# The first weight sums of the twice split feed-forward stages: from GpSimd arithmetic to accumulating DMAs, with the second sums on VectorE

## The chip, the cores and the metric

The kernel runs on one core of one Trainium2 chip. The core has TensorE (matrix products), VectorE (elementwise, the profile's DVE), ScalarE (ACT), GpSimd (POOL) and SyncE (SP, which here issues DMAs). The metric is the device time of one execution in microseconds (us).

## The reference

The program is a transformer of two kinds of block on 512 tokens of width 1024, all in float32. Its first block has two layers, and each layer ends in a gated feed-forward network:

```python
D_FF = 2816
f = rmsnorm(h, ln_ffn_pre[layer])
f = (jax.nn.silu(f @ w_ffn_gate[layer]) * (f @ w_ffn_up[layer])) @ w_ffn_down[layer]
h = h + rmsnorm(f, ln_ffn_post[layer])
```

The change concerns the two products `f @ w_ffn_gate` and `f @ w_ffn_up`, in both layers: two stages of the program. A third feed-forward network, in the second block, is computed by other code and isn't touched.

## The kernel before, in words

The function `ffn_up_quarters` makes one stage. The 2816 columns of each of the two weights are taken 256 at a time, in 11 units (`UNITS`), numbered 0 to 10. A unit has two tiles, each of 1024 rows by 256 columns: one from the gate weight (`w1`), one from the up weight (`w2`). SyncE loads them one after the other into a ring of four slots, so the tiles of two units are on the chip at a time; a load waits on `half_done`, which TensorE raises when it has finished with the unit that used the slot.

The products follow Strassen's scheme in Winograd's form: a 2 x 2 block product with seven products of blocks in place of eight. A11 and A12 are the upper and lower 512 rows of the gate tile, A21 and A22 those of the up tile. Four **first sums** of weights are needed: S1 = A21 + A22, S2 = S1 - A11, S3 = A11 - A21 and S4 = A12 - S2, each 128 partitions x 1024 elements. Unit 0 uses this scheme once. In units 1 to 10 each of the seven products (`m`, computed in the order `QUART_ORDER` = 1, 2, 6, 5, 7, 3, 4) is split once more by the same scheme, so each needs four **second sums** of its own weights (`weight_sums` on VectorE, `own_sums` on GpSimd), and has seven inner products (`PARTS` = 1, 2, 4, 5, 6, 7, 3), of which the last four use the second sums. That is 28 matmul instructions to a product and 196 to a unit (line 2008). Products 1, 2 and 4 use plain blocks; 5 uses S1, 6 uses S2, 7 uses S3, 3 uses S4.

In units 1 to 10 GpSimd makes all four first sums (lines 2247, 2249, 2250, 2258) and the second sums of products 5 and 4 (lines 2217 to 2222). VectorE makes the second sums of 1 and 2, of 6, and of 3 and 7 (lines 2118 to 2123); `take` adds a product's result out of PSUM to what is held (line 2132); `combine` finishes two of the four results of a unit (lines 2150 to 2156); `gated_products` multiplies the two halves of a finished unit (lines 2162, 1596). ScalarE copies results out of PSUM (line 2030) and applies silu (line 2019). In the first of these units the token sums are split too (`turn_moving` on VectorE, `turn_last` on GpSimd).

The order of each engine's work is written out by hand: each engine runs its list in order, and semaphores tie the lists together. In a unit `g`, VectorE's list is: second sums of 6; `combine` of the last unit's c12 and c21; `take` c11; second sums of 3 and 7; gated products of the last unit; `take` v2; `take` c22, which needs ScalarE's copy of product 7; `combine` of c11 and c22; second sums of 1 and 2 of unit `g + 1`; `take` c12; a small piece of a norm (line 275). GpSimd starts a unit when product 5 of the unit before is done, since its first sums have one place only:

```python
pool.tensor_tensor(S1, A21, A22, ALU.add).then_inc(s["pooled"], 1)
pool.wait_ge(s["pooled"], pooled(g, 1))
pool.tensor_tensor(S2, S1, A11, ALU.subtract).then_inc(s["pooled"], 1)
pool.tensor_tensor(A21, A11, A21, ALU.subtract).then_inc(s["pooled"], 1)
```

Of the kernel before, what the change touches and what calls it, by code (L numbers as in the profile page):

```python
# [551 lines left out]
def build(nc, a, out, stop=None, consts=None):  # L552
    k = Kit()
    k.a = a
    with ExitStack() as ctx:
# [32 lines left out]
        k.up_count = dict.fromkeys(UP_SIGNALS, 0)  # L588
        k.up, k.down = {x: sem(f"up_{x}") for x in UP_SIGNALS}, {x: sem(f"down_{x}") for x in DOWN_SIGNALS}
# [984 lines left out]
UP_SIGNALS = ("product", "sum", "act_sum", "copied", "added", "centred", "tapped", "gated", "hidden", "pooled")  # L1574
# [260 lines left out]
QUART_ADDS = {"c11": 1, "v2": 2, "c22": 3, "outer": 8, "c12": 9, "all": 14}  # L1835

# [5 lines left out]
def ffn_up_quarters(k, name, nth, w1, w2, c1, c2, lead, aside=None):  # L1842
# [20 lines left out]
    summed = lambda g, n: base["sum"] + len(UP_SUMS) + 12 * (g - 1) + n  # L1863
    copied = lambda g, what: base["copied"] + 2 + 4 * (g - 1) + QUART_COPIES.index(what) + 1
    added = lambda g, what: base["added"] + 14 * g + QUART_ADDS[what]
    turned = lambda n: base["act_sum"] + 4 + 4 * n
    pooled = lambda g, n: base["pooled"] + 12 * (g - 1) + (4 if (g, n) > (1, 7) else 0) + n
    turned_last = base["pooled"] + 11
    gated = lambda u, n: base["gated"] + 2 * u + n
    for what, n in (("product", 13 + 60), ("sum", 8 + 120), ("act_sum", 16), ("copied", 2 + 40), ("added", 14 * UNITS), ("gated", 2 * UNITS),  # L1870
                    ("pooled", 124)):
        k.up_count[what] += n
# [13 lines left out]
    slot_of = {1: 0, 2: 1, 3: 0, 7: 1, 6: 2, 5: 3, 4: 3}  # L1886
    sums_at = lambda m, i: mem["U"] + 1024 * slot_of[m] + 256 * (i - 1)
# [29 lines left out]

    def sync(k, sp):
        for u in range(UNITS):
            for w, c in ((w1, c1), (w2, c2)):  # L1920
                k.sp_stream.load(w[:, :, c + 256 * u:c + 256 * u + 256], KD, 256)

    def tensor(k, pe):
# [52 lines left out]
        def wait_sums(g, m):
            if m in (5, 4):
                pe.wait_ge(s["pooled"], pooled(g, {5: 7, 4: 12}[m]))
            else:
                pe.wait_ge(s["sum"], summed(g, {1: 4, 2: 4, 6: 8, 7: 12, 3: 12}[m]))  # L1980
# [67 lines left out]
    def vector(k, dve):  # L2048
        def first_sums():
            for i, t in UP_SUMS[0:6]:  # L2050
                A11, A12, A21, A22 = quarters(0, t)
                if i == 1:
                    wait_tile(dve, 0, t)
                    ins = dve.tensor_tensor(sums(t, 1), A21, A22, ALU.add)
                elif i == 2:
                    dve.wait_ge(s["sum"], summed0(1, t))
                    ins = dve.tensor_tensor(sums(t, 2), sums(t, 1), A11, ALU.subtract)
                else:
                    ins = dve.tensor_tensor(A21, A11, A21, ALU.subtract)
                ins.then_inc(s["sum"], 1)  # L2060
                yield
# [22 lines left out]

        def turn_moving(n):
            m = (1, 5, 7)[n]
            (o, c), own = moving_at[m], turned_at[m]
            two = (moving_at[(2, 6, 3)[n]][0] - o, 2)
            y = lambda at: strided(k, o + at, two, (c, 2))
            T = lambda i: strided(k, own + 256 * i, (768, 2), (P, 2))  # L2090
            wait_first(dve, *((2, 1), (5, 1), (3, 1))[n])
            dve.wait_ge(s["act_sum"], base["act_sum"] + 4)
# [32 lines left out]
        def take(g, what):  # L2125
# [6 lines left out]
            dve.tensor_tensor(hold(g, to), hold(g, to), pair(pair_of(g, m)), ALU.add).then_inc(s["added"], 1)  # L2132
# [78 lines left out]
    def pool(k, pool):  # L2211
        def own_sums(g, m, n):
            o, at = halves(g, m), sums_at(m, 1)
            x = lambda off: strided(k, o + off, (256, 2))
            T = lambda i: strided(k, at + 256 * (i - 1), (P, 2))
            done = pooled(g, n)
            pool.tensor_tensor(T(1), x(P), x(512 + P), ALU.add).then_inc(s["pooled"], 1)
            pool.tensor_tensor(T(3), x(0), x(P), ALU.subtract).then_inc(s["pooled"], 1)
            pool.wait_ge(s["pooled"], done + 1)
            pool.tensor_tensor(T(2), T(1), x(0), ALU.subtract).then_inc(s["pooled"], 1)  # L2220
            pool.wait_ge(s["pooled"], done + 3)
            pool.tensor_tensor(T(4), x(512), T(2), ALU.subtract).then_inc(s["pooled"], 1)

        def turn_last():
            (o, c), own = moving_at[4], turned_at[4]
            y = lambda at: strided(k, o + at, (c, 2))
            T = lambda i: strided(k, own + 256 * i, (P, 2))
            wait_first(pool, 4, 1)
            pool.wait_ge(s["act_sum"], base["act_sum"] + 4)
            pool.tensor_tensor(T(0), y(P), y(0), ALU.subtract).then_inc(s["pooled"], 1)  # L2230
            pool.wait_ge(s["pooled"], turned_last - 3)
            pool.tensor_tensor(T(1), y(2 * c + P), T(0), ALU.subtract).then_inc(s["pooled"], 1)
            pool.tensor_tensor(y(P), y(2 * c + P), y(P), ALU.subtract).then_inc(s["pooled"], 1)
            pool.wait_ge(s["pooled"], turned_last - 2)
            pool.tensor_tensor(T(2), y(2 * c), T(1), ALU.subtract).then_inc(s["pooled"], 1)

        for g in range(1, UNITS):
            A11, A12, A21, A22 = (M[:, halves(g, m):halves(g, m) + 1024] for m in (1, 2, 7, 4))
            S1, S2 = (M[:, halves(g, m):halves(g, m) + 1024] for m in (5, 6))
            for t in range(2):  # L2240
                wait_tile(pool, g, t)
            if g == 1:
                wait_first(pool, 5, 1)
                pool.wait_ge(s["sum"], summed0(4, 1))
            else:
                wait_product(pool, g - 1, 5)
# [7 lines left out]
            if g == 1:  # L2254
# [396 lines left out]
def diff_projection(k, lead):  # L2651
# [353 lines left out]
def rwkv_projection(k):  # L3005
# [905 lines left out]
def final_phase(k, out, post):  # L3911
# [3 lines left out]
    turned, copied, last_copied = k.turned, k.turn_read, k.sem("final_last_copied")  # L3915
# [112 lines left out]
```

## Time and profile before

| What | us |
|---|---|
| median of 3 runs (2699.95 to 2705.44) | 2703.03 |
| the profiled execution's own time | 2704.21 |
| its span, first to last instruction | 2702.3 |
| TensorE busy, matmuls (91% of the span) | 2469.5 |
| VectorE busy (59%) | 1598.3 |
| ScalarE busy (21%) | 574.7 |
| GpSimd busy (18%) | 476.9 |
| units 1 to 10 of the first stage, from the first to the last matmul | 266.95 to 566.55 |
| the same of the second stage | 1069.18 to 1368.70 |

A row of the timeline gives the start, the duration, the engine (PE for matmuls, PEld for weight loads), the line of the code, the operation, and in square brackets the time for which the engine had sat idle and what ended it. Matmuls overlap, so the busy time of a single one is longer than its share of the stream. The granted clock of TensorE (PEclk) is 1.00 at 2.4 GHz and 0.50 at 1.2 GHz.

### The profile page before, as it was taken

Reading aid. Unit: us, or ns where it says so; the run is one execution under the profiler, and the core shown is the slowest. Engines: PE = TensorE matmul, PEld = TensorE weight load, DVE = VectorE, ACT = ScalarE, POOL = GpSimd, SP = SyncE. Lnnn points to the kernel's source line nnn. Section 1 sums busy time; section 2 is a strip of 40 time slices with the busy share of each in tenths; the row PEclk is TensorE's granted clock in tenths of the full one; section 3 lists DMA queues with packets and bytes.
Section 4 is the critical chain, followed back from the end, with each engine's and each line's share of the span. In section 5 each row is a group of like instructions: output and inputs, shape, how many; then the busy total and the mean of one; then the engine's idle time right before and its main releaser. Section 6 shows DMA issues by size and latency. Waiting matters only on the chain.

```text
span 2702.3 us, 49191 instructions
## 1 busy us (share of the span) xinstructions
PE 2469.5 (91%) x21352; PEld 1983.5 (73%) x21352; DVE 1598.3 (59%) x2605; ACT 574.7 (21%) x1086; POOL 476.9 (18%) x354
## 2 busy tenths in 40 slices
PE   8998888799999998887899898999888899999998
PEld 5945888788687546887898575445888855888887
DVE  4636877772534527777773456555666535777733
ACT  1121111110102421111110104322444222222201
POOL 0003555500000003555400000001332300000000
PEclk9998888899999999888899998999999999999999
DMA  4433211223322013122123420210000023222232
GB/s 163 124 102 125 64 63 64 84 65 86 109 68 75 1 47 110 63 73 83 54 65 86 147 77 16 71 45 1 4 3 4 4 69 120 94 90 69 72 86 74
DMA packets 222190, 190.53 MB, mean 71 GB/s; under 512 B 8711, under 2 KB 220072, under 8 KB 221976
## 3 DMA queue, kind: packets, MB, share of 16 engines
q1 hardware_dynamic: 221682, 187.29, 22.4%
q8 instruction: 170, 2.79, 0.4%
q14 instruction: 44, 0.36, 0.0%
q10 hardware_dynamic: 294, 0.09, 0.0%
HBM read 185.25 MB, written 2.10 MB: 69 GB/s over the span
## 4 chain that ended last, share of the span: by engine, by line
PE 78%; DVE 15%; issue 3%; ACT 2%; SPq 1%; POOL 1%; DMA 0%; POOLq 0%; DVEq 0%; ACTq 0%
PE psum L2338 14%; PE psum L2008 12%; PE psum L1683 10%; PE psum L517 7%; PE psum L3237 6%; PE psum L1354 4%; PE psum L1350 4%; PE psum L1137 4%; PE psum L3792 2%; DVE sbuf L2153 2%; DVE sbuf L2151 2%; PE psum L1073 1%; PE psum L539 1%; PE psum L3244 1%; DVE sbuf L2119 1%
## 5 line engine op out<-in xcount | busy, mean ns | idle before, releaser
L2008 PE MATMUL psum<-sbuf 128*128 128x128 f32 x3920 | 490.2, 292 | 115.6 <-DVE sbuf L2123 106.4
L2008 PEld LDWEIGHTS psum<-sbuf 128*128 128x128 f32 x3920 | 485.5, 208 | 120.7 <-DVE sbuf L2123 110.2
L2338 PE MATMUL psum<-sbuf 128*128 128x256 f32 x1716 | 371.0, 379 | 0.8 <-DVE sbuf L2366 0.8
L2338 PEld LDWEIGHTS psum<-sbuf 128*128 128x128 f32 x1716 | 325.9, 190 | 45.5 <-issue 1.1
L432 POOL TENSOR_TENSOR sbuf<-sbuf 128x512 f32<-128x512 f32 x30 | 37.8, 1278 | 1352.9 <-DVE sbuf L418 1352.6
L1683 PE MATMUL psum<-sbuf 128*128 128x256 f32 x1232 | 267.7, 380 | 1.7 <-ACT sbuf L493 1.7
L1683 PEld LDWEIGHTS psum<-sbuf 128*128 128x128 f32 x1232 | 235.1, 191 | 34.0 <-issue 1.9
L3237 PE MATMUL psum<-sbuf 64*64 64x64 f32 (+1 forms) x5952 | 212.6, 225 | 33.2 <-DVE sbuf L3629 10.2
L3237 PEld LDWEIGHTS psum<-sbuf 64*64 64x64 f32 x5952 | 197.7, 137 | 45.0 <-issue 26.5
L517 PE MATMUL psum<-sbuf 128*128 128x512 f32 (+3 forms) x560 | 203.9, 521 | 0.3 <-issue 0.3
L2030 ACT ACTIVATE sbuf<-psum 128x896 f32<-128x896 f32 x80 | 73.3, 917 | 481.0 <-PE psum L2008 313.8
L3694 POOL TENSOR_TENSOR sbuf<-sbuf 128x512 f32<-128x512 f32 x60 | 74.9, 1270 | 549.1 <-DVE sbuf L3618 518.7
L517 PEld LDWEIGHTS psum<-sbuf 128*128 128x128 f32 (+2 forms) x560 | 103.4, 186 | 92.4 <-issue 87.0
L2132 DVE TENSOR_TENSOR sbuf<-sbuf,psum 128x896 f32<-128x896 f32 x80 | 86.7, 1083 | 101.5 <-ACT sbuf L2030 56.5
L2390 DVE TENSOR_TENSOR sbuf<-sbuf,psum 128x256 f32<-128x256 f32 x84 | 33.5, 418 | 189.6 <-PE psum L2338 189.2
L1354 PE MATMUL psum<-sbuf 128*128 128x256 f32 (+2 forms) x536 | 122.3, 389 | 0.0
L1354 PEld LDWEIGHTS psum<-sbuf 128*128 128x128 f32 x536 | 99.1, 190 | 23.5 <-issue 3.2
L1137 PE MATMUL psum<-sbuf 128*128 128x512 f32 x256 | 115.7, 601 | 0.6 <-DVEq L623 0.6
L1350 PEld LDWEIGHTS psum<-sbuf 128*128 128x128 f32 x1008 | 113.8, 192 | 2.8 <-issue 2.4
L1350 PE MATMUL psum<-sbuf 128*128 128x128 f32 x1008 | 113.8, 275 | 0.0
L1767 DVE TENSOR_TENSOR sbuf<-sbuf,psum 128x256 f32<-128x256 f32 x154 | 59.2, 416 | 68.9 <-PE psum L1683 68.9
L1412 DVE TENSOR_TENSOR sbuf<-sbuf,psum 128x256 f32<-128x256 f32 (+1 forms) x119 | 53.4, 450 | 70.8 <-PE psum L1354 39.5
(326 smaller groups left out, 3539.2 us busy)
## 6 DMA issues: line engine op xcount, KB each, us to landing
sbuf<-in_w_mod_dram SPq DMA_DIRECT2D x24, 1024.0 KB, 5.2
sbuf<-in_w_ffn_gate_dram SPq DMA_DIRECT2D x22, 1024.0 KB, 5.4
sbuf<-in_w_ffn_up_dram SPq DMA_DIRECT2D x22, 1024.0 KB, 5.5
sbuf<-in_w_ffn_down_dram SPq DMA_DIRECT2D x32, 704.0 KB, 5.3
sbuf<-in_w_up_dram SPq DMA_DIRECT2D x22, 1024.0 KB, 7.3
sbuf<-in_w_out_dram SPq DMA_DIRECT2D x12, 1024.0 KB, 6.7
sbuf<-in_w_in_dram SPq DMA_DIRECT2D x12, 1024.0 KB, 5.8
sbuf<-in_w_down_dram SPq DMA_DIRECT2D x16, 704.0 KB, 6.5
```

Source lines behind the costliest of these rows:

```text
L517: mm = pe.matmul(bank, w[:, q, c0:c0 + m], rhs(k0 + q), start=start and q == 0, stop=stop and q == kc - 1)
L1137: mm = pe.matmul(bank_of(b), tiles[b // 2][:, q, (b % 2) * P:(b % 2) * P + P], MIX[:, q, :], start=q == 0, stop=q == KD - 1)
L1350: mm = pe.matmul(self.bank(p)[:, t * P:(t + 1) * P], x[:, q, :], w[:, q, :], start=q == 0, stop=q == 3)
L1354: mm = pe.matmul(self.bank(p)[:, c0:c1], w[:, q, :], x[:, q, :], start=q == 0, stop=q == 3)
L1683: mm = pe.matmul(bank, w[:, q, :], rhs[:, q, :], start=q == 0, stop=q == 3)
L1767: dve.tensor_tensor(out, base, bank_of(u, p, t), ALU.add).then_inc(s["added"], 1)
L2008: mm = pe.matmul(k.psum[:, at:at + P], weights(g, m, p, q), moving(m, p, q), start=q == 0 and p in (1, 2) and m in (1, 2, 5, 3), stop=q == ...
L2030: act.activation(hold(g, to), pair(pair_of(g, m)), ACT.Copy).then_inc(s["copied"], 1)
L2132: dve.tensor_tensor(hold(g, to), hold(g, to), pair(pair_of(g, m)), ALU.add).then_inc(s["added"], 1)
L2338: mm = pe.matmul(bank_of(g, p), wt[:, q, :], rhs_of[p][:, q, :], start=q == 0, stop=q == UNITS - 1)
L3237: mm = pe.matmul(out[h], lhsT[h], rhs[h], start=start, stop=stop)
L3694: pool.tensor_tensor(split(LOFF[lv]), split(GB[g % 2][:, :, 0, :]), both_level(lv), ALU.mult).then_inc(sems["loff"], 1)
```

## The change

The signs of the scheme are moved so that each first sum is an addition to something that is in place. The first token block is negated (`negate_first`), the token sums and two of the four `take`s subtract the other way round, and the first sums become S1 = A21 + A22, S2 = S1 + A11, S3 = A21 + A11, S4 = A12 + S2. For units 1 to 10 of both stages:

- SyncE copies A21 and A11 from the chip's main memory a second time, into the places of S1 and S2 (two DMAs of 128 x 1024 elements, 512 KB each).
- GpSimd does no arithmetic in the stage. Its queue issues four accumulating DMAs to a unit, which add a source to what stands at the destination: A11 from main memory onto A21 (S3), A22 from main memory onto the copy of A21 (S1), S1 onto the copy of A11 (S2), and S2 onto A12 (S4). Each is 512 KB. GpSimd waits for each landing that the next one needs.
- VectorE makes all second sums, of products in pairs: 1 and 2, 5 and 6, 7 and 4, and 3 alone. `turn_last` moves to VectorE as a fourth `turn_moving`.
- The places of the second sums alternate between odd and even units (`slot_of`), and some semaphores are shared with other stages.

```diff
+    def quarter_in(w, c, g, h):
+        return w[:, 4 * h:4 * h + 4, c + 256 * g:c + 256 * g + 256]
+    def quarter_at(g, m):
+        return view(M, halves(g, m), 4, 256)
     def sync(k, sp):
-        for u in range(UNITS):
+        def load(u):
             for w, c in ((w1, c1), (w2, c2)):
                 k.sp_stream.load(w[:, :, c + 256 * u:c + 256 * u + 256], KD, 256)
+        load(0)
+        for g in range(1, UNITS):
+            load(g)
+            if g == 1:
+                wait_first(sp, 5, 1)
+                sp.wait_ge(s["sum"], summed0(4, 1))
+            else:
+                wait_product(sp, g - 1, 5)
+                wait_landed(sp, g - 1, "S4")
+            sp.dma_start(quarter_at(g, 5), quarter_in(w2, c2, g, 0)).then_inc(k.sum_landed["S1 copy"], 16)
+            sp.dma_start(quarter_at(g, 6), quarter_in(w1, c1, g, 0)).then_inc(k.sum_landed["S2 copy"], 16)
...
         def weight_sums(g, n):
-            m, then = ((1, 2), (6, None), (3, 7))[n]
+            m, then = ((1, 2), (5, 6), (7, 4), (3, None))[n]
...
+            elif n == 1:
+                wait_landed(dve, g, "S1")
+                wait_landed(dve, g, "S2")
+                if g >= 2:
+                    wait_product(dve, g - 1, 4)
+            elif n == 2:
+                wait_tile(dve, g, 1)
+                wait_landed(dve, g, "S3")
+                wait_product(dve, g, 2)
             else:
-                dve.wait_ge(s["pooled"], pooled(g, {1: 2, 2: 8}[n]))
-                if n == 2:
-                    wait_product(dve, g, 2)
-                elif g >= 2:
-                    wait_product(dve, g - 1, 6)
+                wait_landed(dve, g, "S4")
+                wait_product(dve, g, 5)
...
-            dve.tensor_tensor(hold(g, to), hold(g, to), pair(pair_of(g, m)), ALU.add).then_inc(s["added"], 1)
+            if what in ("c11", "c12"):
+                ins = dve.tensor_tensor(hold(g, to), pair(pair_of(g, m)), hold(g, to), ALU.subtract)
+            else:
+                ins = dve.tensor_tensor(hold(g, to), hold(g, to), pair(pair_of(g, m)), ALU.add)
+            ins.then_inc(s["added"], 1)
...
             weight_sums(g, 2)
-            if g >= 2:
+            if g == 1:
+                turn_moving(3)
+            else:
                 gated_products(g - 1)
             take(g, "v2")
+            weight_sums(g, 3)
             take(g, "c22")
...
     def pool(k, pool):
...
         for g in range(1, UNITS):
-            pool.tensor_tensor(S1, A21, A22, ALU.add).then_inc(s["pooled"], 1)
-            pool.wait_ge(s["pooled"], pooled(g, 1))
-            pool.tensor_tensor(S2, S1, A11, ALU.subtract).then_inc(s["pooled"], 1)
-            pool.tensor_tensor(A21, A11, A21, ALU.subtract).then_inc(s["pooled"], 1)
-            if g >= 2:
-                wait_product(pool, g - 1, 4)
-            own_sums(g, 5, 3)
-            if g == 1:
-                turn_last()
-            wait_product(pool, g, 2)
-            pool.wait_ge(s["pooled"], pooled(g, 2))
-            pool.tensor_tensor(A12, A12, S2, ALU.subtract).then_inc(s["pooled"], 1)
-            wait_product(pool, g, 5)
-            own_sums(g, 4, 8)
+            wait_tile(pool, g, 1)
+            pool.dma_start(quarter_at(g, 7), quarter_in(w1, c1, g, 0), accum_op=ALU.add).then_inc(k.sum_landed["S3"], 16)
+            wait_landed(pool, g, "S1 copy")
+            pool.dma_start(quarter_at(g, 5), quarter_in(w2, c2, g, 1), accum_op=ALU.add).then_inc(k.sum_landed["S1"], 16)
+            wait_landed(pool, g, "S2 copy")
+            wait_landed(pool, g, "S1")
+            pool.dma_start(quarter_at(g, 6), quarter_at(g, 5), accum_op=ALU.add).then_inc(k.sum_landed["S2"], 16)
+            wait_landed(pool, g, "S2")
+            wait_product(pool, g, 2)
+            pool.dma_start(quarter_at(g, 3), quarter_at(g, 6), accum_op=ALU.add).then_inc(k.sum_landed["S4"], 16)
```

GpSimd's list for one unit, before (first the second sums that follow product 5 of the unit, at the end the first sums of the next one):

```order
L2258 TENSOR_TENSOR sbuf<-sbuf 128x1024 [waits up_pooled,up_product]
L2217 TENSOR_TENSOR sbuf<-sbuf 128x256 [waits up_product]
L2218 TENSOR_TENSOR sbuf<-sbuf 128x256
L2220 TENSOR_TENSOR sbuf<-sbuf 128x256 [waits up_pooled]
L2222 TENSOR_TENSOR sbuf<-sbuf 128x256 [waits up_pooled]
L2247 TENSOR_TENSOR sbuf<-sbuf 128x1024 [waits up_product,tile_landed2,tile_landed1]
L2249 TENSOR_TENSOR sbuf<-sbuf 128x1024 [waits up_pooled]
L2250 TENSOR_TENSOR sbuf<-sbuf 128x1024
```

The same list with the change; `x_in0` and `x_in1` count the landings of the two copies, `sum_landed0` and `sum_landed1` those of S1 and S2:

```order
L2254 DMA sbuf<-in_w_ffn_gate_dram 128x4x256 [waits tile_landed2]
L2256 DMA sbuf<-in_w_ffn_up_dram 128x4x256 [waits x_in0]
L2259 DMA sbuf<-sbuf 128x1024 [waits sum_landed0,x_in1]
L2262 DMA sbuf<-sbuf 128x1024 [waits up_product,sum_landed1]
```

All arithmetic has left GpSimd's list, and three of its four DMAs wait for a landing.

VectorE's list with the change, from the second `take` of a unit (lines 2164 and 2166 are the two forms of `take`) to the first `combine` of that unit:

```order
L2166 TENSOR_TENSOR sbuf<-sbuf,psum 128x896
L2149 TENSOR_TENSOR sbuf<-sbuf 128x256
L2150 TENSOR_TENSOR sbuf<-sbuf 128x256
L2152 TENSOR_TENSOR sbuf<-sbuf 128x256
L2154 TENSOR_TENSOR sbuf<-sbuf 128x256
L2166 TENSOR_TENSOR sbuf<-sbuf,psum 128x896
L2185 TENSOR_TENSOR sbuf<-sbuf 128x2x128
L2186 TENSOR_TENSOR sbuf<-sbuf 128x2x128
```

Before, the two `take`s stood next to each other; the second sums of product 3 now stand between them.

## Rows read from the trace of the kernel before

**Rows 1.** Page, costliest groups: matmuls of the two stages, and `combine`'s rows in 260 to 560

```profile
L2008 PE MATMUL psum<-sbuf 128*128 128x128 f32 x3920 | 490.2, 292 | 115.6 <-DVE sbuf L2123 106.4
...
L2151 DVE TENSOR_TENSOR sbuf<-sbuf 128x256 f32<-128x256 f32 x18 | 24.7, 1374 | 0.0
```

**Rows 2.** Timeline of one unit of the first stage, all engines, from one TensorE wait to the next

```profile
359.39 24.48 PE L2008 MATMUL psum<-sbuf 128*128 128x128 f32 x196 [5.97 <-DVE sbuf L2123]
...
376.38 0.92 ACT L2030 ACTIVATE sbuf<-psum 128x896 f32<-128x896 f32 x1 [5.34 <-PE psum L2008]
377.33 1.09 DVE L2132 TENSOR_TENSOR sbuf<-sbuf,psum 128x896 f32<-128x896 f32 x1 [2.75 <-ACT sbuf L2030]
378.45 0.49 DVE L2150 TENSOR_TENSOR sbuf<-sbuf 128x256 f32<-128x256 f32 x1
378.74 2.42 POOL L2249 TENSOR_TENSOR sbuf<-sbuf 128x1024 f32<-128x1024 f32 x1
378.87 2.57 DVE L2151 TENSOR_TENSOR sbuf<-sbuf 128x256 f32<-128x256 f32 x1
...
386.12 1.21 DVE L2118 TENSOR_TENSOR sbuf<-sbuf 128x512 f32<-128x512 f32 x1
...
389.83 24.42 PEld L2008 LDWEIGHTS psum<-sbuf 128*128 128x128 f32 x196 [6.15 <-DVE sbuf L2123]
```

**Rows 3.** The same timeline, VectorE where GpSimd is idle: second sums, `combine`, gated products

```profile
360.59 0.42 DVE L2118 TENSOR_TENSOR sbuf<-sbuf 128x256 f32<-128x256 f32 x1
...
362.05 0.42 DVE L2150 TENSOR_TENSOR sbuf<-sbuf 128x256 f32<-128x256 f32 x1
362.39 0.42 DVE L2151 TENSOR_TENSOR sbuf<-sbuf 128x256 f32<-128x256 f32 x1
...
364.17 0.42 DVE L2156 TENSOR_TENSOR sbuf<-sbuf 128x256 f32<-128x256 f32 x1
...
369.37 0.69 DVE L2118 TENSOR_TENSOR sbuf<-sbuf 128x512 f32<-128x512 f32 x1 [1.27 <-POOL sbuf L2258]
...
371.91 1.22 DVE L2162 TENSOR_TENSOR sbuf<-sbuf 128x1024 f32<-128x1024 f32 x1
...
373.50 1.08 DVE L2132 TENSOR_TENSOR sbuf<-sbuf,psum 128x896 f32<-128x896 f32 x1
```

**Rows 4.** Windows, line 2008 alone: stretch, its us; PE busy (count), PEld busy (count); PEclk; DMA share; GB/s

```profile
366.00:378.00 12.00, 12.00 (x110) 12.00 (x109) 1.00 0.01 1
359.40:363.40 4.00, 4.00 (x19) 4.00 (x19) 0.50 0.00 0
...
299.40:303.00 3.60, 3.54 (x17) 3.54 (x18) 0.53 0.22 69
```

**Rows 5.** DMA issues: KB each, median us from issue to landing

```profile
sbuf<-in_w_ffn_gate_dram SPq DMA_DIRECT2D x22, 1024.0 KB, 5.4
...
sbuf<-in_mem_dram SPq DMA_DIRECT2D x1, 1024.0 KB, 12.7
```

**Rows 6.** Windows, all engines (PE, PEld, DVE, ACT, POOL busy and counts; PEclk; DMA share; GB/s), during a load

```profile
381.50:383.00 1.50, 1.50 (x16) 1.50 (x15) 1.50 (x1) 0.00 (x0) 1.50 (x1) 1.00 1.00 350
```

**Rows 7.** Page, DMA queues: packets, MB, share of 16 engines

```profile
q1 hardware_dynamic: 221682, 187.29, 22.4%
q8 instruction: 170, 2.79, 0.4%
q14 instruction: 44, 0.36, 0.0%
q10 hardware_dynamic: 294, 0.09, 0.0%
```

**Rows 8.** Timelines, first stage: unit 0's matmuls, GpSimd's first sum, first and last full units

```profile
249.67 13.98 PE L1945 MATMUL psum<-sbuf 128*128 128x256 f32 x64
...
253.55 2.56 POOL L2247 TENSOR_TENSOR sbuf<-sbuf 128x1024 f32<-128x1024 f32 x1 [22.81 <-PE psum L1945]
...
299.46 23.76 PE L2008 MATMUL psum<-sbuf 128*128 128x128 f32 x196 [2.77 <-DVE sbuf L2123]
...
543.13 23.42 PE L2008 MATMUL psum<-sbuf 128*128 128x128 f32 x184 [5.95 <-DVE sbuf L2123]
```

**Rows 9.** Timeline of TensorE, last matmuls of units 1 to 10 of the second stage

```profile
1345.30 23.40 PE L2008 MATMUL psum<-sbuf 128*128 128x128 f32 x184 [5.97 <-DVE sbuf L2123]
```

More of the change, by code:

```diff
@@ L588, in build @@
         k.up_count = dict.fromkeys(UP_SIGNALS, 0)
+        k.sum_landed = {x: sem(f"sum_landed{n}") for n, x in enumerate(SUM_SIGNALS[2:])}
+        k.sum_landed.update(zip(SUM_SIGNALS[:2], k.x_in))
+        k.sum_base = {x: 16 if x.endswith("copy") else 0 for x in SUM_SIGNALS}
         k.up, k.down = {x: sem(f"up_{x}") for x in UP_SIGNALS}, {x: sem(f"down_{x}") for x in DOWN_SIGNALS}
@@ L1573 @@
 LAST_READ = {2: "c11", 6: "u2", 5: "c22", 7: "u3", 4: "c21", 3: "c12"}
-UP_SIGNALS = ("product", "sum", "act_sum", "copied", "added", "centred", "tapped", "gated", "hidden", "pooled")
+UP_SIGNALS = ("product", "sum", "act_sum", "copied", "added", "centred", "tapped", "gated", "hidden")
 DOWN_SIGNALS = ("product", "sum", "copied", "added")
@@ L1835 @@
 QUART_ADDS = {"c11": 1, "v2": 2, "c22": 3, "outer": 8, "c12": 9, "all": 14}
+SUM_SIGNALS = ("S1 copy", "S2 copy", "S1", "S2", "S3", "S4")
 def strided(k, off, *dims):
@@ L1862, in ffn_up_quarters @@
     product = lambda g, m: base["product"] + len(UP_ORDER) + 6 * (g - 1) + QUART_ORDER.index(m) + 1
-    summed = lambda g, n: base["sum"] + len(UP_SUMS) + 12 * (g - 1) + n
+    summed = lambda g, n: base["sum"] + len(UP_SUMS) + 16 * (g - 1) + n
     copied = lambda g, what: base["copied"] + 2 + 4 * (g - 1) + QUART_COPIES.index(what) + 1
     added = lambda g, what: base["added"] + 14 * g + QUART_ADDS[what]
-    turned = lambda n: base["act_sum"] + 4 + 4 * n
-    pooled = lambda g, n: base["pooled"] + 12 * (g - 1) + (4 if (g, n) > (1, 7) else 0) + n
-    turned_last = base["pooled"] + 11
+    turned = lambda n: base["act_sum"] + 5 + 4 * n
+    added_in = lambda g, what: k.sum_base[what] + 16 * (10 * nth + g)
     gated = lambda u, n: base["gated"] + 2 * u + n
-    for what, n in (("product", 13 + 60), ("sum", 8 + 120), ("act_sum", 16), ("copied", 2 + 40), ("added", 14 * UNITS), ("gated", 2 * UNITS),
-                    ("pooled", 124)):
+    for what, n in (("product", 13 + 60), ("sum", 8 + 160), ("act_sum", 21), ("copied", 2 + 40), ("added", 14 * UNITS), ("gated", 2 * UNITS)):
         k.up_count[what] += n
@@ L1973, in wait_halves @@
             else:
-                pe.wait_ge(s["pooled"], pooled(g, {6: 2, 5: 1, 7: 3, 3: 8}[m]))
+                wait_landed(pe, g, {6: "S2", 5: "S1", 7: "S3", 3: "S4"}[m])
         def wait_sums(g, m):
[L1977 to L1980, printed above, removed]
+            pe.wait_ge(s["sum"], summed(g, {1: 4, 2: 4, 6: 8, 5: 8, 7: 12, 4: 12, 3: 16}[m]))
         def weights(g, m, p, q):
             o = halves(g, m)
-            at = {1: o + 256 * q, 2: o + 512 + 256 * q, 4: o + 512 + P + 256 * q, 5: sums_at(m, 1) + P * q, 6: sums_at(m, 2) + P * q,
-                  7: sums_at(m, 3) + P * q, 3: sums_at(m, 4) + P * q}[p]
+            at = {1: o + 256 * q, 2: o + 512 + 256 * q, 4: o + 512 + P + 256 * q, 5: sums_at(g, m, 1) + P * q, 6: sums_at(g, m, 2) + P * q,
+                  7: sums_at(g, m, 3) + P * q, 3: sums_at(g, m, 4) + P * q}[p]
             return M[:, at:at + P]
@@ L2083, in first_add, with negate_first @@
                 dve.tensor_tensor(out, of, bank_of(p, t), ALU.add).then_inc(s["added"], 1)
+        def negate_first():
+            wait_first(dve, 1, 1)
+            dve.wait_ge(s["act_sum"], base["act_sum"] + 4)
+            dve.tensor_scalar(B[0], B[0], -1.0, None, ALU.mult).then_inc(s["act_sum"], 1)
+            dve.wait_ge(s["act_sum"], turned(0))
         def turn_moving(n):
-            m = (1, 5, 7)[n]
+            m, then, last = ((1, 2, (2, 1)), (5, 6, (5, 1)), (7, 3, (3, 1)), (4, None, (4, 1)))[n]
             (o, c), own = moving_at[m], turned_at[m]
[L2088 to L2092, printed above, removed]
+            two = ((moving_at[then][0] - o, 2),) if then else ()
+            next_two = ((768, 2),) if then else ()
+            y = lambda at: strided(k, o + at, *two, (c, 2))
+            T = lambda i: strided(k, own + 256 * i, *next_two, (P, 2))
+            wait_first(dve, *last)
             dve.tensor_tensor(T(0), y(P), y(0), ALU.subtract).then_inc(s["act_sum"], 1)
@@ L2100, in weight_sums @@
         def weight_sums(g, n):
-            m, then = ((1, 2), (6, None), (3, 7))[n]
-            o, own = halves(g, m), sums_at(m, 1)
-            two = ((halves(g, then) - o, 2),) if then else ()
-            next_two = ((1024, 2),) if then else ()
+            m, then = ((1, 2), (5, 6), (7, 4), (3, None))[n]
+            o, own = halves(g, m), sums_at(g, m, 1)
+            two = ((1024, 2),) if then else ()
             x = lambda at: strided(k, o + at, *two, (256, 2))
-            T = lambda i: strided(k, own + 256 * (i - 1), *next_two, (P, 2))
+            T = lambda i: strided(k, own + 256 * (i - 1), *two, (P, 2))
             if n == 0:
@@ L2165, in vector @@
         first = first_sums()
-        t1, t2, t3, t4 = token_sums(dve, B, [TA[:, i] for i in range(3)])
-        t1().then_inc(s["act_sum"], 1)
+        B11, B12, B21, B22 = B
+        T1, T2, T4 = (TA[:, i] for i in range(3))
+        dve.tensor_tensor(T1, B12, B11, ALU.subtract).then_inc(s["act_sum"], 1)
         next(first)
         dve.wait_ge(s["act_sum"], base["act_sum"] + 1)
-        t2().then_inc(s["act_sum"], 1)
+        dve.tensor_tensor(T2, B22, T1, ALU.subtract).then_inc(s["act_sum"], 1)
         for _ in range(3):
             next(first)
-        t3().then_inc(s["act_sum"], 1)
+        dve.tensor_tensor(B12, B12, B22, ALU.subtract).then_inc(s["act_sum"], 1)
         next(first)
         dve.wait_ge(s["act_sum"], base["act_sum"] + 2)
-        t4().then_inc(s["act_sum"], 1)
+        dve.tensor_tensor(T4, B21, T2, ALU.subtract).then_inc(s["act_sum"], 1)
         next(first)
@@ L2179, in vector @@
         first_add("c11")
+        negate_first()
         turn_moving(0)
@@ L2211, in pool @@
     def pool(k, pool):
[L2212 to L2235, printed above, removed]
```

38 lines of the change are left out of this document (15 added, 23 removed).

## The prediction

> **What bounds the kernel now.** I read four views: the costliest groups for the size of the loss, the timeline of one unit for its cause, the windows for TensorE's pace and clock, and the DMA views for what a transfer costs. Times are us.
>
> In the costliest groups the matmuls of the two stages have 115.6 of idle time before them, 106.4 of it ended by line 2123, the last of VectorE's second sums [rows 1]. The timeline of one unit shows it: TensorE resumes at 359.39 and at 389.83, 30.4 apart, and sits idle for 5.97 of that [rows 2]. The unit from wait to wait has 196 matmuls, and the last unit of a stage has 184 from its wait to the end [rows 8]: 12 are missing, so the wait stands behind the first 12 of product 1, where its second sums are first needed.
>
> Read the rows between the two resumptions as a loop: TensorE does the rest of 1, then 2, 6, 5 and 7 (128 matmuls, to 376.38); ScalarE copies 7; VectorE takes c22 at 377.33, runs `combine`, makes the second sums, and TensorE goes on at 389.83. VectorE is slow in it: line 2151 takes 2.57 beside GpSimd's 2.42 of line 2249, and line 2118 takes 1.21 beside GpSimd's second sums [rows 2]; with GpSimd idle the same shapes take 0.42 and 0.69 [rows 3]. GpSimd's arithmetic thus costs VectorE's piece of the loop, from 378.45 to 389.83, 11.4. Undisturbed, `combine` takes 2.5 (362.05 to the end of line 2156 at 364.59) and the four sums 2.5 (369.37 to 371.91) [rows 3].
>
> The idle time also lowers the clock. After the pause that ended at 359.39 the granted clock is 0.50 (1.2 GHz), 19 matmuls in 4.00; from 366 on it is 1.00 (2.4 GHz), 110 in 12.00 [rows 4]. I take 0.11 for one at the full clock: 21.6 for a unit of 196.
>
> **What goes.** GpSimd's arithmetic, and with it VectorE's delay. The loop becomes 128 x 0.11 = 14.1, plus ScalarE 0.9, `take` 1.1, `combine` 2.5 and sums 2.5: 21.1, less than TensorE's own 21.6. VectorE gains work: the second sums of product 5 join those of 6 in instructions twice as long (2.5 in place of 1.5), and 4 joins 7 in the place of 3, which gets four instructions of its own (1.5, from 360.59 to 362.05 [rows 3]). Its unit is then three sets of sums of 2.5, one of 1.5, two `combine` of 2.5, four `take` of about 1.0, gated products 1.6 (371.91 to 373.50 [rows 3]) and 0.3 for the norm's piece: 20. That is below 21.6, so VectorE doesn't bound, if nothing disturbs it. `negate_first` and the fourth `turn_moving`, once per stage, lie in unit 1 beside the DMAs and cost nothing; without that cover they would add some 3 per stage.
>
> **What comes: a chain of transfers.** SyncE may copy for the next unit when product 5 is done and S4 has landed; GpSimd adds to the copy for S1; when that landed, S1 for S2; then VectorE makes the sums of 5 and 6; then TensorE runs the rest of product 6 and product 5, and SyncE may copy again. Each link waits for the one before. On SyncE's queue the next tile loads stand behind these copies; they need `half_done` from a later product of the same unit, so the copies hold them up only if S4 is very late. On GpSimd's queue the S3 of the next unit stands between S4 and S1; it runs while the copy is under way.
>
> The price of a link. A tile load of 1024 KB (1.05 MB) lands after 5.4 [rows 5]; under way it moves 350 GB/s with the DMA engines fully busy [rows 6], 3.0 for its bytes, so 2.4 is fixed. A copy of 512 KB costs 2.4 + 1.5 = 3.9; the second copy hides behind the S1 transfer. No row shows an accumulating DMA, nor a queue of GpSimd's [rows 7]. From below it is a plain copy, 3.9; from above the slowest row, a load that took 12.7 in company [rows 5]. I take 2.4 + 1.5 + 1.5 = 5.4, since the destination must be read as well. It is nearer the low end, because that row is of the same kind and stage, and the high one fell into the start of the program, among many loads. For what GpSimd itself does to issue one I add nothing, since no row shows it; the upper bound stands for it.
>
> Company comes here too: the two tile loads of a unit, 2.1 MB, keep the DMA engines busy for 6.0. They are released at the first matmul of product 4 and at the end of the unit, 7 to 10 after product 5, just when the S2 transfer starts (3.9 + 5.4 = 9.3 after it). If each side gets every other turn, S2's 3.0 of work takes 6.0: S2 costs 8.4.
>
> The rule that speaks for less: the Trainium skill, "DMA: Bandwidth & Descriptors", section "Anatomy of one DMA — SWDGE (gpsimd) path", gives 2.0 us plus the bytes over 436 GB/s for a DMA of GpSimd's queue, 3.2 for these by an estimate from it. By its form 1.05 MB would take 4.4, where the trace has 5.4, so I don't take it; by it the chain would be 3.9 + 3.2 + 3.2 + 7.5 = 17.8, and all of it hidden. The same page, section "Rules for kernel authors", says that an accumulating DMA reads its destination and writes it later; no row here shows it.
>
> **The sum.** One turn of the chain: copy 3.9, S1 5.4, S2 8.4, sums 2.6, rest of product 6 (16 x 0.11) 1.8, product 5 (28 x 0.11) 3.1: 25.2. TensorE waits about 3 in each turn; after a wait of 2.77 it had 0.53 of the clock for 3.60 [rows 4, 8]. Most of that passes under VectorE's 2.6, so I add 0.4: **25.6 per unit**. The other ring, S4 landed, copy, S1, S2, S4, is 3.9 + 5.4 + 8.4 + 5.4 = 23.1 and doesn't bind.
>
> First stage: unit 0's product 5 lets GpSimd start at 253.55 [rows 8]. Copy, S1, S2 (the loads fall in here too), sums, 6 and 5 bring product 5 of unit 1 to 253.6 + 25.2 = 278.8. TensorE arrives earlier: 263.65 (end of unit 0 [rows 8]) plus four products, 12.3, is 276. Nine turns: 278.8 + 230.4 = 509.2. Then products 7, 3 and 4, 84 x 0.11 = 9.2, and 0.8 for the sums of product 3, which VectorE has 12.7 after S2 landed (2.6 + 2.5 + 1.0 + 2.5 + 1.6 + 1.0 + 1.5), where TensorE needs them at 11.9: end at 519.2. Before it was 543.13 + 23.42 = 566.55 [rows 8]: 47 less. The second stage is the same program (its last 184 matmuls take 23.40 [rows 9]): 94 in all. The profiled execution took 2704.2, so the forecast is **2610**; the median of the runs is 1.2 below that execution, which is no more than their spread.
>
> **Rivals.**
> - *All transfers hidden.* If an accumulating DMA costs a plain copy's 3.9 and loads don't disturb it, the chain is 3.9 + 7.8 + 7.5 = 19.2, and TensorE's 21.6 plus the 0.8 at product 3 binds: 22.4. Product 5 of unit 1 at 277, the end at 277 + 201.6 + 10.0 = 488.6: 78 per stage, **2548**. For it: the loads use the engines for 6.0 only. Against: the change adds six transfers of 0.52 MB to a unit, four of which read twice; that is 3.0 + 4 x 3.0 more, with the loads 21 of the DMA engines' time in a turn of 25. This is where the skill's formula leads.
> - *The transfers are the new bound, and slower.* The turn before is 30.4; the chain (3.9 + 2 L + 7.5, and 2 for the clock after a long wait) passes it at L = 8.5 per accumulating DMA, the ring of S4 (3.9 + 3 L) at 8.8. With L = 10 the ring gives 33.9; product 5 of unit 1 comes at 285, the end at 285 + 305 + 10 = 600, 34 later per stage: **2772**. With the bound of 12.7 on all three the ring is 42.0 and the end at about 680, 113 later, 2931. For it: three dependent landings in a row on a queue that no row prices. Against: L must be 1.6 above the 6.9 that my S1 and S2 average with the loads' company.
> - *No net change.* If GpSimd holds VectorE up while it issues DMAs, as its arithmetic did, the old loop stays at about 30: **2700**. For it: VectorE beside GpSimd is slow in any shape [rows 2]. Against: none of GpSimd's list is arithmetic any more.
>
> **How the numbers follow.** Forecast case 0.41, all hidden 0.24, slower 0.31, no change 0.04. Faster by over 0.2% (5.4, about what a measurement of this kernel can tell) is the first two: 0.65; within 0.2%: 0.04; slower: 0.31. The range goes from 2540, just under the hidden case (TensorE's bare 21.6 would give about 2530), to 2775, the slower case with L = 10; beyond it lie the rest of the slower cases, about 0.13, and under it about 0.05. Of the faster cases alone the range would be 2545 to 2660.
>
> **What would show it.** In the profile after: a DMA queue of GpSimd's with 80 issues, some 42 MB; 21 MB more on SyncE's; GpSimd almost without busy time between 240 and 570; line 2151's successor at about 0.42 in place of 1.37; the wait of TensorE moved from the second sums of product 1 to those of product 6, about 3 long, ended by VectorE's sums that waited on S2; a turn of 25.6; an accumulating DMA at 5 to 8 from issue to landing. The forecast is wrong if a DMA of GpSimd's needs over 8.5, if VectorE's sums stay above 1 beside GpSimd, or if TensorE's wait is found at product 3, behind S4.

## The result and the profile after

The changed kernel takes 2666.70 us (median of 4 runs, 2664.11 to 2674.97) against 2701.49 for the kernel before (median of 4 runs): a ratio of 0.9875, 95% interval 0.9849 to 0.9901. It is faster, by 34.8 us where 94 was forecast; the measured time lies inside the stated range, and the gain is little over a third of the one forecast. Two of the executions below ran with TensorE at a low clock throughout, e5 (3262.13 us at 0.72) and one of e7's four (3989.67 us at 0.58); their times aren't used, and e8 repeats e5.

Page of the changed kernel, costliest groups and DMA queues, in the columns of [rows 1] and [rows 7] (line 2028 is the matmul that was line 2008):

```profile
q1 hardware_dynamic: 242802, 208.27, 25.4%
q0 software_dynamic: 26880, 41.95, 9.5%
...
L2028 PE MATMUL psum<-sbuf 128*128 128x128 f32 x3920 | 487.7, 290 | 83.2 <-DMA sbuf<-sbuf 78.9
```

TensorE's idle time before these matmuls fell from 115.6 only to 83.2, and a DMA now ends nearly all of it. The new queue carries 41.95 MB, as the 80 issues should.

Timeline of one turn, TensorE, SyncE's issues (SPq) and GpSimd's, to be read beside [rows 2]:

```profile
383.11 2.09 PE L2028 MATMUL psum<-sbuf 128*128 128x128 f32 x12 [3.93 <-DMA sbuf<-sbuf]
...
385.73 23.23 PE L2028 MATMUL psum<-sbuf 128*128 128x128 f32 x184 [0.53 <-DVE sbuf L2154]
...
393.36 0.36 SPq L1946 DMA_DIRECT2D sbuf<-in_w_ffn_up_dram  x1
...
397.53 1.29 POOL L2256 DMA_DIRECT2D sbuf<-in_w_ffn_up_dram  x1 [12.08 <-DMA sbuf<-in_w_ffn_up_dram]
...
399.83 0.37 SPq L113 DMA_DIRECT2D sbuf<-in_w_ffn_gate_dram  x1
...
402.74 0.37 SPq L113 DMA_DIRECT2D sbuf<-in_w_ffn_up_dram  x1
...
404.83 0.89 POOL L2259 DMA_DIRECT2D sbuf<-sbuf  x1 [6.02 <-DMA sbuf<-in_w_ffn_up_dram]
...
413.30 24.48 PE L2028 MATMUL psum<-sbuf 128*128 128x128 f32 x196 [4.34 <-DMA sbuf<-sbuf]
```

The reader sees the chain of the forecast: product 5 done and the copy issued (393.36), S1 (397.53), S2 (404.83), product 6 (413.30). The two tile loads start at 399.83 and 402.74, so most of their traffic lies beside S2. The wait stands ahead of product 6, 3.9 to 4.3 long.

The chain of waits of the same stretch (start, us, what):

```profile
393.36 3.89 DMA sbuf<-in_w_ffn_up_dram
397.25 0.28 issue
397.53 6.74 DMA sbuf<-in_w_ffn_up_dram
...
404.31 0.53 issue
404.83 8.33 DMA sbuf<-sbuf
413.16 0.14 issue
413.30 8.86 PE psum L2028 x56
```

Copy 3.89, S1 6.74, S2 8.33, and 0.95 of hand-overs between them (from a landing to the next issue or matmul) that no row of before could show. The turn in the steady part of the first stage (unit 2's wait at 298.34 to unit 9's at 497.48, seven turns) is 28.45; before it was 30.4 [rows 2]. In the second stage it is 28.9 (nine turns, 1051.89 to 1311.78).

Windows of the changed kernel, columns as in [rows 6]:

```profile
393.40:405.00 11.60, 11.60 (x107) 11.60 (x105) 9.88 (x17) 1.83 (x2) 1.46 (x2) 1.00 0.79 206
...
413.30:417.00 3.70, 3.70 (x17) 3.68 (x18) 3.63 (x7) 0.00 (x0) 2.21 (x2) 0.50 0.64 118
```

After the wait TensorE runs at 0.50 of its clock, 17 matmuls in 3.70. Where the stage begins shows how much of the gain lies in it. Timelines of TensorE, the first matmuls of unit 0 of the first stage, before and after:

```profile
237.11 25.25 PE L1945 MATMUL psum<-sbuf 128*128 128x256 f32 x106 [0.93 <-DVE sbuf L481]
```

```profile
232.60 26.70 PE L1971 MATMUL psum<-sbuf 128*128 128x256 f32 x112 [0.93 <-DVE sbuf L481]
...
537.52 5.18 PE L2028 MATMUL psum<-sbuf 128*128 128x128 f32 x44 [0.39 <-DVE sbuf L2154]
```

The stage took 566.55 - 237.11 = 329.4 before and 542.70 - 232.60 = 310.1 now, 19.3 less; the second one went from 329.3 (1039.42 to 1368.70) to 313.5 (1016.09 to 1329.63), 15.7 less. The 35.0 of both are the whole difference of the medians. The two profiled executions differ by 39.4; 4.5 of that lies ahead of the first stage, whose first matmul comes at 232.60 in place of 237.11, and its cause isn't known here.

And VectorE is no longer held up. One of its groups in 260 to 543:

```profile
L2186 DVE TENSOR_TENSOR sbuf<-sbuf 128x256 f32<-128x256 f32 x19 | 7.9, 417 | 0.0
```

That is the row that took 1374 ns [rows 1].

### The profile page after: what moved, and what is told of

The parts are those of the page before. It is cut to its first block, busy times and chain, and to the rows that moved or that the text cites. A ratio compares the mean times of both kernels' runs of the same rounds, so it can differ in the third digit from the quotient of the medians.

```text
span 2662.8 us, 49191 instructions
## 1 busy us (share of the span) xinstructions
PE 2463.7 (93%) x21352; PEld 1978.9 (74%) x21352; DVE 1520.5 (57%) x2695; ACT 573.6 (22%) x1086; POOL 215.0 (8%) x186
## 3 DMA queue, kind: packets, MB, share of 16 engines
q0 software_dynamic: 26880, 41.95, 9.5%
## 4 chain that ended last, share of the span: by engine, by line
PE 74%; DMA 13%; DVE 6%; issue 4%; ACT 1%; SPq 1%; POOL 1%; POOLq 0%; DVEq 0%; ACTq 0%
PE psum L2340 14%; PE psum L1686 10%; DMA sbuf<-in_w_ffn_up_dram 8%; PE psum L517 7%; PE psum L2028 6%; PE psum L3239 6%; DMA sbuf<-sbuf 5%; PE psum L1357 5%; PE psum L1353 4%; PE psum L1140 4%; PE psum L3794 2%; PE psum L1971 1%; PE psum L1076 1%; PE psum L3246 1%; PE psum L2790 1%
## 5 line engine op out<-in xcount | busy, mean ns | idle before, releaser
L2028 PE MATMUL psum<-sbuf 128*128 128x128 f32 x3920 | 487.7, 290 | 83.2 <-DMA sbuf<-sbuf 78.9
L1686 PEld LDWEIGHTS psum<-sbuf 128*128 128x128 f32 x1232 | 235.4, 191 | 34.2 <-issue 2.0
L2149 DVE TENSOR_TENSOR sbuf<-sbuf 128x512 f32<-128x512 f32 x80 | 49.4, 618 | 156.1 <-issue 143.8
```

The lines of the kernel that those rows point to most:

```text
L1686: mm = pe.matmul(bank, w[:, q, :], rhs[:, q, :], start=q == 0, stop=q == 3)
L2028: mm = pe.matmul(k.psum[:, at:at + P], weights(g, m, p, q), moving(m, p, q), start=q == 0 and p in (1, 2) and m in (1, 2, 5, 3), stop=q == ...
```

## The experiments

My theory after the result: the chain of copy, S1 and S2 sets the turn, and each of its terms was a little too low. The rival causes were VectorE's longer list, the accumulating DMA's own price, the company of the tile loads, and the clock.

**e1: without the first sums.** All six DMAs of a unit and the waits on them are gone.

```diff
-            sp.dma_start(quarter_at(g, 5), quarter_in(w2, c2, g, 0)).then_inc(k.sum_landed["S1 copy"], 16)
-            sp.dma_start(quarter_at(g, 6), quarter_in(w1, c1, g, 0)).then_inc(k.sum_landed["S2 copy"], 16)
...
     def wait_landed(eng, g, what):
-        eng.wait_ge(k.sum_landed[what], added_in(g, what))
+        return
```

> This kernel leaves out the first sums of units 1 to 10: both copies, all four accumulating DMAs and every wait on them; the products use what stands in those places. Theory (the transfers' chain sets the turn of 28.5 us in the changed kernel, and the old loop is gone): the turn falls to 22.4 us, TensorE's 21.6 plus 0.8 at product 3, and the time to about 2558 us. Rival (VectorE's longer list binds): the turn stays at 24 us or more and the time at 2587 us or more.

Measured: 2533.12 us (one execution). Timeline, TensorE, the first stage:

```profile
258.88 219.03 PE L2020 MATMUL psum<-sbuf 128*128 128x128 f32 x1960
```

All 1960 matmuls in one piece, 21.9 a unit, without a wait: VectorE's new list is no bound, and even the 0.8 at product 3 that I had reckoned isn't there; the time is 25 under the theory's. About 2533 (one execution) is what the program takes when the first sums cost nothing.

**e2: the wait filled with matmuls.**

```diff
+                if m == 6:
+                    spare = k.psum[:, 1024 * pair_of(g, m) + SPAN:1024 * pair_of(g, m) + 1024]
+                    for _ in range(13):
+                        pe.matmul(spare, k.ident, k.means, start=False, stop=True, skip_group_check=True)
                 wait_halves(g, m)
```

> 13 matmuls of constants into unused PSUM columns (2.9 us at full clock) stand ahead of product 6, in TensorE's wait for S2. Theory (the clock after the pause costs the chain 1.5 us per turn): the granted clock stays at 1.00 after the wait, the piece from S2's landing to the end of product 5 falls from 9.0 to 7.5 us, the turn from 28.5 to 27.0, the time to about 2638 us. Rival (the clock passes under VectorE's sums and costs nothing, the transfers set all): the turn stays at 28.5 and the time at 2662 to 2670 us.

Measured: 2646.11 us, ratio 0.9797 (0.9777 to 0.9817). Windows of e2, columns as above, and its chain of waits from S2's landing on:

```profile
390.00:420.00 30.00, 28.15 (x248) 27.57 (x246) 22.93 (x41) 5.93 (x8) 5.20 (x5) 1.00 0.85 209
```

```profile
380.42 0.69 DVE sbuf L2154
...
383.09 5.19 PE psum L2033 x44
...
388.30 3.77 DMA sbuf<-in_w_ffn_up_dram
```

The clock stays at 1.00, and from S2's landing to the next copy it is 7.9 (380.42 to 388.30) in place of 8.9 (413.30 to 422.17 in the changed kernel). By means over nine turns of the first stage it is 7.9 and 8.9 too. The turn is 27.6 (eight turns from 269.20 to 489.86). The clock's share is thus about 0.9 of the turn, where the theory said 1.5 and the prediction 0.4, and 20 us of the time. The chain stays the bound.

**e3: the tile loads held back.**

```diff
+            if g + 1 < UNITS:
+                wait_landed(sp, g, "S2")
+                load(g + 1)
```

> The tile loads of unit g + 1 wait until S2 of unit g has landed, so that no load runs beside S1 and S2. Theory (the loads' company makes S1 and S2 dear): S1 takes 5.5 to 6 us from issue to landing and S2 about 5 in place of 8.9, the turn falls to about 24.5, the time to about 2595 us. Rival (an accumulating DMA costs this by itself): S2 stays above 8 us, and the time at 2665 us, or above it if the later loads now make TensorE wait for tiles.

Measured: 2633.23 us, ratio 0.9745 (0.9726 to 0.9764), a turn of 27.1 (eight turns from 292.79 to 509.27). The two SBUF-to-SBUF transfers, by line, with all 20 issues of each: first the changed kernel (S2 in line 2259, S4 in 2262),

```profile
L2259 POOL DMA_DIRECT2D sbuf<-sbuf x20: 882/886/936, 259.7 to 1303.9; - x20
...
DMA to landing us min/median/max: 6.1/8.9/9.9
```

```profile
L2262 POOL DMA_DIRECT2D sbuf<-sbuf x20: 852/861/861, 269.0 to 1311.9; - x20
...
DMA to landing us min/median/max: 4.5/4.7/5.4
```

then e3 (S2 in line 2262, S4 in 2265):

```profile
L2262 POOL DMA_DIRECT2D sbuf<-sbuf x20: 882/886/896, 260.8 to 1277.6; - x20
...
DMA to landing us min/median/max: 4.5/4.5/6.1
```

```profile
L2265 POOL DMA_DIRECT2D sbuf<-sbuf x20: 852/861/863, 267.1 to 1282.4; - x20
...
DMA to landing us min/median/max: 4.5/9.6/10.6
```

The company of the loads is shown: 4.4 for S2, which falls from 8.9 to 4.5. But the loads now run beside S4, which rises from 4.7 to 9.6, and the other ring takes over, from one S4 to the next. The chain of waits of e3:

```profile
399.58 9.52 DMA sbuf<-sbuf
...
409.16 4.52 DMA sbuf<-in_w_ffn_up_dram
...
413.97 6.62 DMA sbuf<-in_w_ffn_up_dram
...
421.15 6.10 DMA sbuf<-sbuf
427.25 0.28 issue
427.53 9.57 DMA sbuf<-sbuf
```

S4 9.5, copy 4.5, S1 6.6, S2 6.1 (above its median in this turn) and 1.2 of hand-overs make the turn of 27.95, and TensorE isn't in it. The theory was right on S2 and wrong on the time, since it left out where the loads would go. S1 didn't get cheaper without loads (6.0 before, 6.8 here by medians), but this run doesn't give its price alone: S3 is now issued just ahead of it, in all but the first unit of a stage 1.5 to 4.5 us. In e4, without the second copy, S1 takes 6.1, and in no run with adding less than 5.7.

**e4: S2 on VectorE.** The copy for S2 and its accumulating DMA go; VectorE adds S1 and A11.

```diff
-            sp.dma_start(quarter_at(g, 6), quarter_in(w1, c1, g, 0)).then_inc(k.sum_landed["S2 copy"], 16)
...
-            pool.dma_start(quarter_at(g, 6), quarter_at(g, 5), accum_op=ALU.add).then_inc(k.sum_landed["S2"], 16)
...
+                S1, S2, A11 = (M[:, halves(g, i):halves(g, i) + 1024] for i in (5, 6, 1))
+                dve.tensor_tensor(S2, S1, A11, ALU.add).then_inc(k.sum_landed["S2"], 1)
+                wait_landed(dve, g, "S2")
```

> VectorE makes S2 = S1 + A11 with one instruction of 128 x 1024 elements (1.25 us); the copy for S2 and its accumulating DMA are gone. Theory: the chain is 4.2 + 6.5 + 1.3 + 2.6 + 4.9 = 19.5 us, shorter than TensorE's 21.6, so the turn falls to about 22.5 and the time to about 2560 us. Rival (VectorE, with 21.3 us of work in a turn and in strict order, becomes the bound): the turn is 24 to 25 us and the time 2587 to 2605 us.

Measured: 2536.56 us (4 runs, 2534.22 to 2538.85), ratio 0.9392 (0.9378 to 0.9406). Timeline, TensorE, first stage:

```profile
258.52 17.16 PE L2027 MATMUL psum<-sbuf 128*128 128x128 f32 x152
276.02 120.86 PE L2027 MATMUL psum<-sbuf 128*128 128x128 f32 x1080 [0.35 <-DVE sbuf L2156]
397.40 1.57 PE L2027 MATMUL psum<-sbuf 128*128 128x128 f32 x12 [0.51 <-DVE sbuf L2141]
399.96 9.64 PE L2027 MATMUL psum<-sbuf 128*128 128x128 f32 x84 [0.99 <-DVE sbuf L2156]
410.01 70.84 PE L2027 MATMUL psum<-sbuf 128*128 128x128 f32 x632 [0.40 <-DVE sbuf L2156]
```

One instruction of 1.22 in the place of a transfer of 8.9, with the copy for it gone too, took the chain under TensorE's own time: 2.25 of waiting is left in the stage, and the time is 3.4 us from e1's, well under the theory's 2560. Nothing is left out in this kernel, and of those that leave nothing out it is the fastest: 6.1% under the one before.

**e5 and e8: the same DMAs without adding.** GpSimd's four transfers copy (`accum_op` left out).

> GpSimd's four DMAs copy and no longer add; the additions of all first sums of units 1 to 10 are left out. Theory (an addition makes the DMA engines read the destination as well, 1.5 us more of their time for each): S4, which runs nearly alone, falls from 4.7 to about 3.5 us from issue to landing, S1 from 6.0 to 5.0, S2 from 8.9 to 7.0; the turn falls from 28.5 to 25.5 and the time to about 2612 us. Rival (GpSimd's queue and the landing make the price, adding is free): S4 stays within 0.3 of 4.7, the time at 2660 to 2670 us.

> The same kernel as e5, whose execution had TensorE at 0.72 of its clock in all stages, so that its time can't be compared: GpSimd's four DMAs copy and no longer add; the additions of all first sums of units 1 to 10 are left out. Theory (the addition is what makes these DMAs dear, by the destination's reading): prices as in e5, S4 3.1 us, S1 4.2 us from issue to landing, issues of 0.55 and 0.76 us; the chain falls from 28.5 to about 23 us, the turn is TensorE's 22 to 23 us and the time 2540 to 2565 us. Rival (those prices were low only because the slow TensorE left the DMA engines idle): S1 above 5 us, S2 above 6.5 us, the time above 2600 us.

Measured (e8): 2557.93 us, ratio 0.9468 (0.9449 to 0.9487). Page of e8, GpSimd's queue, and S4 by line:

```profile
q0 software_dynamic: 11520, 41.95, 4.9%
```

```profile
L2262 POOL DMA_DIRECT2D sbuf<-sbuf x20: 541/547/549, 265.8 to 1210.0; - x20
...
DMA to landing us min/median/max: 2.8/2.9/4.8
```

For the same bytes the queue's share is 4.9% of 2557.5, 1.57 of all engines for each of the 80; with adding it was 9.5% of 2662.8, 3.16. The packets more than double. S4, with no load beside it and only the next unit's S3 behind it, falls from 4.7 to 2.9, S1 from 6.0 to 4.2, S2 from 8.9 to 6.0, and the issue rows from 0.86 to 0.55 and from 1.29 to 0.76. Adding thus costs 1.8 of landing there, 0.3 of that in GpSimd's issue. Copies nearly hide (the forecast's rival said 2548): TensorE waits for S2 in 5 of the 20 units, 5.2 in all, where with adding it waited in each, 78.9 in all. The additions are what doesn't hide. The Trainium skill, "DMA: Bandwidth & Descriptors", section "Anatomy of one DMA — SWDGE (gpsimd) path", has a fit that gives 3.2 here by an estimate from it; that lies between the copies' 2.9 and 4.2 and under the additions' 4.5 at best. Whether the reading of the destination is all of the difference, these runs don't tell.

**e6: one part of the change alone.** VectorE's new list is kept; GpSimd makes the four first sums by arithmetic.

```diff
-            pool.dma_start(quarter_at(g, 7), quarter_in(w1, c1, g, 0), accum_op=ALU.add).then_inc(k.sum_landed["S3"], 16)
...
+            pool.tensor_tensor(S1, A21, A22, ALU.add).then_inc(k.sum_landed["S1"], 1)
+            pool.tensor_tensor(S2, S1, A11, ALU.add).then_inc(k.sum_landed["S2"], 1)
+            pool.tensor_tensor(A21, A21, A11, ALU.add).then_inc(k.sum_landed["S3"], 1)
...
+            pool.tensor_tensor(A12, A12, S2, ALU.add).then_inc(k.sum_landed["S4"], 1)
```

> One part of the change alone: VectorE makes all second sums in the new order, but GpSimd makes the four first sums by arithmetic as before (no copies, no accumulating DMAs). Theory (GpSimd's arithmetic holds VectorE up, instruction against instruction): GpSimd works 9.6 us in a turn, VectorE's rows beside it take 2.4 to 2.7 us, the turn is 26 to 28 us and the time 2625 to 2660 us. Rival (only GpSimd's second sums did harm): the turn is 22.5 to 23.5 us, the time 2560 to 2578 us.

Measured: 2653.69 us, ratio 0.9831 (0.9815 to 0.9847), a turn of 27.5 (seven turns from 316.80 to 509.31). Timeline of e6, where GpSimd's three sums follow product 5:

```profile
393.94 2.41 POOL L2256 TENSOR_TENSOR sbuf<-sbuf 128x1024 f32<-128x1024 f32 x1
394.07 2.57 DVE L2142 TENSOR_TENSOR sbuf<-sbuf 128x256 f32<-128x256 f32 x1
396.32 2.52 POOL L2257 TENSOR_TENSOR sbuf<-sbuf 128x1024 f32<-128x1024 f32 x1
396.56 2.56 DVE L2144 TENSOR_TENSOR sbuf<-sbuf 128x256 f32<-128x256 f32 x1
...
399.64 23.70 PE L2020 MATMUL psum<-sbuf 128*128 128x128 f32 x196 [3.83 <-DVE sbuf L2146]
```

Two of GpSimd's sums each hold up one instruction of VectorE for their whole length, as in [rows 2], in the second sums of product 3; TensorE waits for these. Over the seven turns VectorE is busy for 185.86 of 192.51 us: it is the bound here. Still this is faster than the changed kernel: its interval ends at 0.9847, and that of the change begins at 0.9849, so the two are only just apart. Taken in this order, the second sums' move to VectorE thus brought more than the whole gain, about 46 us, and the six transfers in place of four sums of 2.4 gave some 12 of it back. What the transfers would do with the old second sums no run shows.

**e7: S1 and S2 on VectorE.** No copies; GpSimd's queue adds S3 and S4 only.

```diff
+                dve.tensor_tensor(S1, A21, A22, ALU.add).then_inc(k.sum_landed["S1"], 1)
+                wait_landed(dve, g, "S1")
+                dve.tensor_tensor(S2, S1, A11, ALU.add).then_inc(k.sum_landed["S2"], 1)
+                wait_landed(dve, g, "S2")
```

> VectorE makes S1 and S2 (two instructions of 128 x 1024 elements); no copies, GpSimd's queue adds only S3 and S4. Theory (with S2 alone on VectorE TensorE is nearly the bound; 1.25 us more puts VectorE at 22.6 us in a turn, above TensorE's 21.9): the turn is about 23, the time 2550 to 2560 us, slower than with S2 alone. Rival (fewer DMAs and no copy to wait for help more than VectorE's work costs): the time is 2536 us or less.

Measured: 2547.87 us (median of 3 runs, 2542.95 to 2549.10), ratio 0.9432 (0.9416 to 0.9448), a little under the theory's 2550 and slower than e4, as it said. Windows of e7 over seven turns:

```profile
303.44:461.18 157.74, 155.06 (x1372) 153.73 (x1372) 154.86 (x246) 34.78 (x48) 15.26 (x14) 1.00 0.57 141
```

A turn is 22.5, and VectorE is busy for 154.86 of 157.74: here it is the bound.

## Why the prediction was right in sign and wrong in size

- **What bounded the kernel before** was read rightly: GpSimd's arithmetic beside VectorE's. With it gone the rows are back at 0.42 and 0.69. But the prediction took this arithmetic as one cost: by e6 it was the second sums whose leaving paid, and transfers in place of the first sums lost some 12 us.
- **VectorE's new list** (20 in a turn) hides, as forecast: e1. The 0.8 at product 3 isn't there in e1, but 0.35 to 0.40 of it is in the timeline of e4, in two of ten units. The cover for `negate_first` and the fourth `turn_moving` held: e1 runs through unit 1 without a wait.
- **The chain as the new bound** and the place of the wait were right. The wait is 3.9 on average (78.9 over 20 units, from 2.4 to 5.5), where the prediction had about 3. Right too was the time of the DMA engines for an accumulating DMA, 3.0 by the sum and 3.16 by the queue's share.
- **What failed is the sum's step "25.6 per unit".** The turn was 28.45, 2.85 more. By medians of the changed kernel: copy with its hand-over 4.2 (forecast 3.9); S1 6.0 and 0.55 of hand-over (5.4); S2 8.9 and 0.1 (8.4); from there to the next copy the rest, 8.7 (7.9). None is far off. They lie in a ring, so each 0.1 counts eighteen times (nine turns in two stages), and all four erred to the same side.
- The largest of the four is **S1, "5.4"**, short by 1.15: I priced it as a load that also reads its target, and added nothing for what GpSimd does. Its issue alone takes 1.29, and the hand-over to the next 0.53. By kind, the hand-overs, which the sum put at nothing, are 0.95 of the 2.85, the most of all. Of the last piece's 0.8 the clock is 0.5: I put 0.4 for it, and e2 gives 0.9.
- **S2, "8.4"** was near (8.9), but by luck, since two errors offset each other. e3 shows the company to be 4.4, where I had 3.0, on a transfer that costs 4.5 alone, where I had 5.4.
- **Term by term**, from unit 0's first matmul, in the first stage: S2 of unit 1 landed at 36.2 (forecast 271.3 - 237.1 = 34.2), nine turns took 256.0 (230.4), and the end came 17.8 after the last wait (17.5). That is 27.9 more than forecast, 310.1 in place of 282.1, and nine tenths of it are the turns.
- **The rivals.** The slower case needed 8.5 for each accumulating DMA; S2 has that and more, as one of the prediction's own signs of being wrong had it, but S1 and S4 don't, and the turn stayed under the 30.4 of before. The hidden case is what e4 reaches and e8 nearly does. Nothing is left of the case without a net change.

## What to carry to other kernels

Price a chain of transfers that closes on itself as a ring, with the issue and the hand-over of every link, and ask of each link whether an engine with some time left could make it: one VectorE instruction of 1.22 us replaced a transfer of 8.9 and the copy ahead of it, worth 130 us here, although VectorE looked nearly full. A change that moves two things should be taken apart: here the one brought 46 us and the other cost 12. Holding other traffic back helps the link beside it and burdens the next; see first where that traffic will go.

## What the runs showed that I hadn't expected

An accumulating DMA of 512 KB from SBUF to SBUF cost 4.5 us from issue to landing with no load beside it (S2 in e3), 4.7 with another one issued behind it (S4), against 2.9 for S4 as a plain copy on the same queue. On average over the four of a unit it took 3.16 us of all DMA engines, as a copy 1.57. It was issued in 0.86 us where both sides are rows of 1024 elements, and in 1.29 where the source is four pieces of 256 (S1); as copies these took 0.55 and 0.76. And a VectorE instruction with two SBUF inputs that met one of GpSimd's could wait for nearly all of it: 2.57 us in place of 0.42 beside one of 2.41. A `take` in e6, with one input in PSUM, kept its 1.08 beside one of 2.36.
